# A hybrid decoder step on one core: sample tokens on a path of their own, the paged attention spread over the stages, key pages turned by VectorE

## What is computed

```python
def _conv_layer(x, state, g, w_in, w_conv, w_out):              # layer A
    b, c, u, z = jnp.split(_rmsnorm(x, g) @ w_in, 4, axis=-1)
    v = c * u
    ext = jnp.concatenate([state.astype(v.dtype), v], axis=1)
    ...
    y = (jax.nn.silu(z) * b * conv) @ w_out
    return x + y, ext[:, -(CONV_W - 1):]

def _fox_attend(q, fq, qpos, k, v, fk, kpos):
    s = jnp.einsum('nqhd,nkhd->nhqk', q, k).astype(jnp.float32) * (HEAD_DIM ** -0.5)
    s = s + (jnp.transpose(fq, (0, 2, 1))[:, :, :, None]
             - jnp.transpose(fk, (0, 2, 1))[:, :, None, :])
    ...
    p = jax.nn.softmax(s, axis=-1)
    return jnp.einsum('nhqk,nkhd->nqhd', p.astype(v.dtype), v)

def _fox_layer(x, attend, g, w_in, g_q, w_out):                 # layer B
    q, z = jnp.split(_rmsnorm(x, g) @ w_in, 2, axis=-1)
    q = _rmsnorm(q.reshape(N, L, N_HEADS, HEAD_DIM), g_q)
    o = attend(q).reshape(N, L, D_ATTN)
    return x + (o * jax.nn.silu(z)) @ w_out
```

## Time and profile before

| | |
|---|---|
| time, median of 3 runs | 976.64 us (974.82 to 976.98) |
| span of the profiled execution | 973.7 us; its own time is not listed apart, the median lies 2.9 us above the span |
| TensorE, matmuls | 935.6 us busy, 8516 instructions |
| VectorE, ScalarE, GpSimd | 489.1, 384.8, 168.3 us busy |
| moved by DMA | 206.4 MB, 212 GB/s on average |

### The profile page before, as it was taken

The page is one execution under the profiler, slowest core; times in us unless marked ns, Lnnn a source line. Parts: engine busy times, 40 slices in busy tenths (PEclk is TensorE's granted clock), DMA queues, the critical chain, the costliest instruction groups (busy, mean ns, idle before and its releaser), DMA issues.

```text
span 973.7 us, 23729 instructions
## 1 busy us (share of the span) xinstructions
PE 935.6 (96%) x8516; PEld 798.8 (82%) x8516; DVE 489.1 (50%) x1133; ACT 384.8 (40%) x728; POOL 168.3 (17%) x111
## 2 busy tenths in 40 slices
PE   3899999999999999999999999999999999999998
PEld 2899999999998997758768768678687687786898
DVE  5744645555256434453554544644535545545732
ACT  5233333332135443453543544535435445436210
POOL 2243444331130221101102002012020020100000
PEclk8799999999999999999999999999999999999999
DMA  6222222322542525879799799798897997986412
GB/s 211 68 85 86 66 87 84 86 86 89 152 150 81 177 87 178 295 253 368 249 334 335 241 361 317 245 372 297 280 356 251 352 336 241 370 317 227 166 44 98
DMA packets 133188, 206.40 MB, mean 212 GB/s; under 512 B 8831, under 2 KB 91312, under 8 KB 133026
## 3 DMA queue, kind: packets, MB, share of 16 engines
q1 hardware_dynamic: 123538, 199.40, 60.7%
q10 hardware_dynamic: 9088, 4.46, 1.7%
q0 software_dynamic: 528, 2.10, 0.8%
HBM read 195.29 MB, written 10.63 MB: 211 GB/s over the span
## 4 chain that ended last, share of the span: by engine, by line
PE 84%; DMA 5%; DVE 4%; ACT 4%; issue 2%; SPq 0%; ACTq 0%; DVEq 0%
PE psum L1224 41%; PE psum L1194 17%; PE psum L1249 9%; PE psum L1382 7%; PE psum L1497 4%; DMA page_ring<-in_cache_k 4%; ACT sample_scores L708 2%; PE psum L1447 2%; DMA w_raw<-in_a_w_out 1%; PE psum L1425 1%; PE psum L1297 1%; PE psum L1405 1%; PE psum L1427 1%; PE psum L1429 1%; DMA constants<-in_table 0%
## 5 line engine op out<-in xcount | busy, mean ns | idle before, releaser
L1224 PE MATMUL psum<-xn_high,w_high 128*128 128x256 f32 x992 | 233.9, 318 | 2.6 <-DVE xn_low L821 2.6
L1224 PE MATMUL psum<-xn_low,w_high 128*128 128x256 f32 x992 | 213.6, 297 | 0.0
L1224 PE MATMUL psum<-xn_high,w_low 128*128 128x256 f32 x992 | 213.5, 297 | 0.0
L1224 PEld LDWEIGHTS psum<-xn_high,w_high 128*128 128x128 f32 x992 | 162.9, 191 | 19.6 <-issue 16.6
L1224 PEld LDWEIGHTS psum<-xn_high,w_low 128*128 128x128 f32 x992 | 168.1, 190 | 0.0
L1224 PEld LDWEIGHTS psum<-xn_low,w_high 128*128 128x128 f32 x992 | 168.0, 190 | 0.0
L1194 PE MATMUL psum<-constants,page_ring 128*128 128x128 f32 x1024 | 136.4, 276 | 6.3 <-DMA page_ring<-in_cache_k 5.0
L1194 PEld LDWEIGHTS psum<-constants,page_ring 128*128 128x128 f32 x1024 | 114.1, 140 | 33.4 <-issue 31.9
L503 POOL TENSOR_TENSOR w_raw<-w_raw,gains 128x1024 f32<-128x1024 f32 x32 | 60.7, 1897 | 339.2 <-DMA w_raw<-in_b_w_in 218.3
L1002 DVE COPY k_turned_odd<-psum 128x512 f32<-128x512 f32 x64 | 44.1, 690 | 93.1 <-PE psum L1194 93.1
L835 DVE TENSOR_TENSOR w_low<-w_raw,w_high 128x1024 fp32r<-128x1024 f32 x32 | 49.6, 1551 | 78.7 <-ACT w_high L565 78.7
(11 more groups left out here) (236 smaller groups left out, 1418.7 us busy)
## 6 DMA issues: line engine op xcount, KB each, us to landing
page_ring<-in_cache_k SPq DMA_DIRECT2D x128, 512.0 KB, 5.6
page_ring<-in_cache_v SPq DMA_DIRECT2D x128, 512.0 KB, 4.7
w_raw<-in_a_w_in SPq DMA_DIRECT2D x32, 512.0 KB, 4.0
suffix<-suffix_scratch SPq DMA_DIRECT2D x32, 256.0 KB, 4.6
w_raw<-in_b_w_in SPq DMA_DIRECT2D x16, 512.0 KB, 5.6
w_raw<-in_kv_w SPq DMA_DIRECT2D x16, 512.0 KB, 6.3
w_raw<-in_a_w_out SPq DMA_DIRECT2D x4, 1024.0 KB, 5.0
f_broad<-f_scratch SPq DMA_DIRECT2D x8, 512.0 KB, 6.0
```

The lines of the kernel that those rows point to most:

```text
L1224: mm = pe.matmul(PS[:, bank + h, 0:c.stop - c.start], w[:, k, :], x[:, k, c], start=(k == 0 and n == 0), stop=(k == KT - 1 and n == 2))
```

## The change

The stages stay, but three things are new.

*The samples leave the prompt's matmuls in the mixer and the queries.* Their rows are now the stationary side: `weights_s` streams 48 weight blocks of 128x1024 (A's input, A's output, the queries' weights) in plain fp32 against 64 columns, ahead of and between the prompt's first channels. So the queries of all samples are there before the mixer's third channel. The prompt's pieces become one matmul of 512 columns. In the heads, key, value and gate projections still run over 576.

*The paged attention follows at once*: sequences 0 to 2 in channels 2 to 7 of the mixer, sequence 3 in the queries, 4 to 7 one for each two pairs of heads. The ring has 16 slots; a value page takes the slot of its key page when that is done with.

*Key pages are turned in place by VectorE*, in blocks of 32x32, and the scores are matmuls on 32x32 tiles that work on these blocks. ScalarE spreads the queries (`spread`).

```diff
--- before.py
+++ after.py
@@ TensorE
-                for p in range(4):
-                    mm = turn(PS[:, T0, p * P:(p + 1) * P], page[:, p * P:(p + 1) * P])
...
+        def weights_s(n, bank):
+            pe.wait_ge(b_page[n % RING], 16 * (n // RING + 1))
+            for h in range(2):
+                mm = pe.matmul(PS[64 * h:64 * h + 64, bank, :], XT[:, n % KT, :], ring[:, n % RING, h * WIDE:(h + 1) * WIDE],
+                               start=(n % KT == 0), stop=(n % KT == KT - 1))
...
+        def piece_a(slot, k, bank):
+            for n, (w, x) in enumerate(((WH, XH), (WH, XL), (WL, XH))):
+                mm = pe.matmul(PS[:, bank, :], w[:, slot, k, :], x[:, k, 0:SEQ],
+                               start=(k == 0 and n == 0), stop=(k == KT - 1 and n == 2))
...
+        def past_scores(r):
+            for h in range(4):
+                for a in range(2):
+                    for j in range(4):
+                        for g in range(4):
+                            c = ((4 * j + h) * 2 + a) * 32
+                            mm = pe.matmul(
+                                PS[32 * j:32 * j + 32, T0 + g, 0:ROUND * 32].rearrange("p (n k) -> p n k", k=32),
+                                QC[32 * g:32 * g + 32, j, 64 * h + 32 * a:64 * h + 32 * a + 32],
+                                ring[32 * g:32 * g + 32, ROUND * r:ROUND * r + ROUND, c:c + 32],
+                                start=(h == 0 and a == 0), stop=(h == 3 and a == 1), tile_position=(32 * g, 32 * j))
...
+        def mixer(i, b):
+            channel(i, 0, range(KT - 1))
+            past_free(b, 0)
+            channel(i, 0, [KT - 1])
+            past_scores(0)
+            channel(i, 1)
+            channel(i, 2, range(KT - 1))
+            past_free(b, 1)
+            channel(i, 2, [KT - 1])
+            past_scores(1)
+            channel(i, 3)
+            past_turns(b)
+            channel(i, 4)
+            past_out(b, range(ROUND), T0, 256)
+            channel(i, 5)
+            past_out(b, range(ROUND, NPG), T0, 256)
...
+                project(e, 0, 0, [5])
+                block_scores(o, 1, 1)
+                project(e, 0, 0, [6, 7])
+                block_turn(o, 0)
+                block_scores(o, 2, 1)
+                project(e, 1, 1, [0, 1])
+                block_out(o, 0)
+                block_turn(o, 1)
@@ VectorE
+        def turn_pages(b, pages):
+            for n in pages:
+                dve.wait_ge(b_page[n], 32 * b + 16 * (S_LOADS + 1))
+                dve.transpose(ring[:, n, :], ring[:, n, :]).then_inc(b_turned, 1)
...
+        def mixer(i, b):
+            turn_pages(b, range(ROUND, 12))
+            take_scores(b, 0)
+            conv(i)
+            turn_pages(b, range(12, NPG))
+            take_scores(b, 1)
...
+                attend(e - 1, (pages(8), keys_e, pages(11, 12), pages(13)))
+                turn_pages(b, (14, 15))
@@ GpSimd
+        def low_b(n, odd, to=None):
+            h, lo = to or (WH[:, odd, :, :], WL[:, odd, :, :])
+            pool.wait_ge(b_high, n + 1)
+            pool.tensor_tensor(lo, WR[:, odd, :, :], h.bitcast(F32), ALU.subtract).then_inc(b_split, 1)
...
+        pool.wait_ge(b_used, NPG * NB)
+        pool.memset(QZ[:, :, :, :], 0.0).then_inc(s_zero, 1)
```

More of the change, by code:

```diff
@@ new lines, in _, with mixer @@
+        spread(0)
+        ahead(0, 6)
+        silu_a(1)
+        ahead(0, 7)
+        gated_high(1)
+        def mixer(i, b, last):
+            ahead(i, 0, last)
+            c_out(i)
+            ahead(i, 1, last)
+            ahead(i, 2, last)
+            silu_a(i)
+            exps(b)
+            ahead(i, 3, last)
+            gated_high(i)
+            probs_out(b)
+            ahead(i, 4, last)
+            c_out(i + 1)
+            spread(b + 1)
+            ahead(i, 5, last)
+            past_out(b, OUT_M)
+            ahead(i, 6, last)
+            silu_a(i + 1)
+            if last:
+                act.wait_ge(l_raw, 16)
+                high_slab(0)
+            ahead(i, 7, last)
+            gated_high(i + 1)
@@ new lines, in _ @@
+        act.wait_ge(s_wfl, 1)
+        for n in (2, 3):
+            load_b(n, n % 2, wqz, n * P)
+        for m in range(KT):
+            query(m)
+            if m == 4:
+                probs_out(3)
+            query_root(m)
+            if m + 4 < KT:
+                load_b(m + 4, m % 2, wqz, (m + 4) * P)
+            elif m + 4 < KT + 2:
+                load_b(m + 4, m % 2, wkv, (0, D)[m % 2])
+            if m == 3:
+                exps(3)
+                spread(4)
+        act.wait_ge(b_proj, KT - 1)
@@ new lines, in _ @@
+        channel(0, 1)
+        pe.wait_ge(y_dve, Y_DVE["ext"])
+        pe.wait_ge(s_cs, H)
+        pe.matmul(PS[:, S_BANK[1], 0:H], CT[:, C_TRI:C_TRI + P], CS[:, :, PAGE - 1], start=True, stop=True).then_inc(s_rtot, 1)
+        pe.wait_ge(y_dve, Y_DVE["gate"])
+        turn_s(S_BANK[2], ZG).then_inc(y_pe, 1)
+        channel(0, 2, range(4))
+        pe.wait_ge(y_dve, Y_DVE["gated"])
+        for n in range(S_IN, S_IN + S_OUT):
+            weights_s(n, S_BANK[0])
+        channel(0, 2, range(4, KT))
@@ L1503, in _, with piece @@
-        with pe.Fori(0, NB) as i:
-            heads(i)
+        past_out(3, range(ROUND), OS, 0)
+        query(6)
+        past_out(3, range(ROUND, NPG), OS, 0)
+        query(7)
+        q_sum(7)
+        pe.wait_ge(q_out, KT)
+        pe.wait_ge(s_fnr, 1)
+        def piece(slot, k):
+            for n, (w, x) in enumerate(((WH, XH), (WH, XL), (WL, XH))):
+                for h in range(2):
+                    c = (slice(0, HALF), slice(HALF, TOK))[h]
+                    mm = pe.matmul(PS[:, D0 + h, 0:c.stop - c.start], w[:, slot, k, :], x[:, k, c],
+                                   start=(k == 0 and n == 0), stop=(k == KT - 1 and n == 2))
+            return mm
```

2142 lines of the change are left out of this document (1260 added, 882 removed).

## The result

| | before | after |
|---|---|---|
| time, median | 976.81 us (974.82 to 977.72) | 1129.8 us (1124.77 to 1136.42) |
| span of the profiled execution | 973.7 | 1130.2 |
| ratio after/before, 95% interval | | 1.1566 [1.1533, 1.1598] |

The change makes the kernel 15.7% slower. The forecast was 965 us with a range up to 1030; it was wrong, in size and in sign. Nothing failed in what the change does: TensorE's page turns are gone and its busy time fell, from 935.6 to 904.4 us. What makes 1130 is TensorE's idle time, 226 us in all (before: 38), and a lower granted clock.

The account below looks back on a forecast made before the run. The prediction took TensorE, busy 935.6 of 973.7 us, as the bound. Its work would fall to about 804 us while idle time rose from 38 to 158; stages summed to 962, with 3 around it 965 us, range 885 to 1030.

Parts of the forecast that it names:

- Page turns: TensorE's work: the 1024 matmuls that turn 128 key pages go, 111 us less.
- sample columns: TensorE's 40 mixer and query projections: one matmul of 512 columns for each piece saves 38 us.
- the samples' path: New TensorE work: 48 weight blocks against 64 stationary columns, at 0.9 us each, 43 us more.
- Scores, 64 us: Paged attention on TensorE: 16 rounds of 128 matmuls on 32x32 tiles, 4.0 us each, 64 us as before.
- Rival E: Score rounds: tiles don't overlap, a round is 16 us, 192 us more; 1155 us, chance 0.04.
- the low clock, charged once with 2.5 us: Start stage: after 9 us idle behind the suffix sums, 12 pieces run at the lower clock, 2.5 us.
- The list of waits: TensorE's waits for other engines, laid out stage by stage: idle time goes from 38 to 158 us.
- Block turn 0: Heads: TensorE waits 6.5 us in a pair for VectorE's divide, which follows maxima, keys' gain and pages.
- Page turn 1.14 us: VectorE's turn of a 128x1024 fp32 key page takes 1.14 us, with bounds of 0.75 to 2.16.
- Rival B: VectorE's page turns run in the fast form at 0.81 us, giving back 19 us; 945 us, chance 0.12.
- Rival C: VectorE's page turns slow beside GpSimd, costing 26 us at 1.55 or 65 at 2.16; 995 us, chance 0.25.
- Rival A: Waits are shorter because queues run ahead, 158 us of idle time becomes 80; 885 us, chance 0.22.

Follow-up runs that it names:

- e3: The changed kernel with each score matmul streaming 128 columns instead of 256, half of the pages' scores left out: 1127.9 us, ratio 1.151 to the kernel before.
- e9: The changed kernel with the score round's tile order swapped, four column groups of one row group one after the other: 1129.1 us, ratio 1.156 to the kernel before.
- e7: The changed kernel with 20 and 22 useless matmuls ahead of the waits for pages and block turn 0: 1121.8 us, ratio 1.149 to the kernel before.
- g1: The changed kernel with three orders turned: division of block 0 earlier, ScalarE's probability copies earlier, page turns 12 to 15 ahead of the convolution: 1098.9 us, ratio 1.120.
- e1: The changed kernel with VectorE's division of block 0 ahead of the keys' gain and page turns 9 and 10: 1097.7 us, ratio 1.121 to the kernel before.
- e4: The changed kernel with 64 instead of 128 matmuls in a score round, part of the scores left out: 1066.2 us, ratio 1.092 to the kernel before.
- e8: The changed kernel with VectorE turning only the first 32 columns of each key page: 1115.2 us, ratio 1.144 to the kernel before.
- e5: The changed kernel with GpSimd making only one eighth of each weight's low half: 1105.6 us, ratio 1.133 to the kernel before.
- b1: The kernel before the change with each 256-column score matmul cut in four of 64, same results: 1036.8 us, ratio 1.061.
- b2: The kernel before the change with each 256-column score matmul cut in two of 128: 981.6 us, ratio 1.005.

## Why the prediction was wrong, point by point

- *Page turns, sample columns, the samples' path.* Right. A piece of 512 columns comes every 0.227 us; 48 blocks cost 49 us for 43. TensorE's work at the full clock is 832 us for 804.
- *Scores, 64 us, "below this it cannot well go".* Mis-sized: 99.6 us, part of it at the low clock; at the full clock a round takes 5.9 us, 23 ns a record for the 16 of the earlier trace rows. That row has 64 columns a matmul; here there are 256, and e3 shows that columns count on these tiles too. The 3.4 us "if columns alone count" come out for 128 matmuls four at a time; by the 256 records the same sum is 6.9. Rival E had named the tiles, with four at a time, 62 ns a record; the 23 lie between. The rule of the Trainium skill that it goes by (TensorE: Matmul & The Clock Gate, Part 3: Packing small matmuls: a weight load overlaps matmuls in flight only where the row group differs) has no support here: e9 puts four column groups of one row group after each other and takes the same 99.7 us.
- *The first step that failed: the low clock, charged once with 2.5 us.* It is the largest part of the 168 us. The clock was low in 36 separate stretches, most of them behind 2 to 8 us of idleness, 73 us in all. The row that says so was the earlier trace rows, and I applied it to one stretch only, though my own list had 156 us of idle time. e7 shows that the low clock follows the idle stretches; how much time comes back without it, no run shows clearly.
- *The second: idle time is what engines wait for each other.* The list of waits had no place for code and put it at nothing. It is 33 us of issue in the changed kernel, nearly all of it behind instruction packets, and more where other waits go: 21 us more of it in g1 than in e1. Rows of before show none of it, since their loop's body is kept (20 packets); I did not count that a body now holds two heads' work, 2330 records for 1310, with 512 of them in each round of 6 us. The rest of the idle time, 193 us, is 37 more than the list had. e4's 64 us are not all part of the miss: 32 of them would have gone by the forecast's own price of the rounds too.
- *Waits in the list.* Block turn 0: 6.5 forecast, 7.8 measured. The page turns are a small part of it (e8: 54 to 47 us over all pairs) and the division, three times as long beside GpSimd, a larger one (e5: 54 to 43); the keys wait 2.0 us for ScalarE's squares, as forecast. Second score round 3.8 and 5.6; the suffix stores' 9 us were a wait of 5.3 near 86 us; spread queries 12 and 11.1; copies of probabilities in a heads pair 4.4 and 2.9.
- *Page turn 1.14 us.* Right: 1.13 from start to start. Rival B's 19 us for the fast form go by 0.4 us a page, where 1.14 less 0.81 is 0.33, so 16.
- *Rival C, pages slow beside GpSimd.* Right side, wrong operation. Turns don't slow; the divisions do (1.62 us on average for 512 columns, 0.48 before), as does one step of the convolution with one input, also 128x512 (2.64 us beside it, 0.49 without). The 2.5 us a page that this rival works out from the Trainium skill (VectorE: DVE Perf Modes, The three transpose paths) did not come: that table's figure is for a 16-bit type, which the prediction does not say, and the fp32 turns took 1.2 us. GpSimd's low half is itself 2.4 us where I took 2.
- *Rival A and the range.* The range ended at 1030, as no case joined the low clock to all waits. That alone, 70 us more on 965, gives 1035.

## What to carry to other kernels

Before trading a few large matmuls for many small ones, count instructions as well as columns: per round, and per loop body. If the body before has few instruction packets and no issue time, it says nothing about a larger one; cutting one group of matmuls finer, results unchanged, tests it in one run (b1). When TensorE's work is cut but idle stretches appear, charge the low clock behind each one of them, and expect a removed wait to uncover the next floor. An idle gap without a releaser is not yet a wait for code: look whether an instruction packet lands in it, and whether another engine ends something just before it does.

## What the runs showed of the hardware

- A loop body of TensorE with 1570 matmul and load records was kept (b2: 21 instruction packets for the run); one with 1697 was fetched anew at each turn (9 packets a turn in the changed kernel's mixer); with 2080, 93 packets came and each turn of the loop stood 5.4 to 6.0 us (b1). Gaps of over 1 us in which TensorE waited for code ended 1.2 to 1.8 us after a packet had landed.
- On 32x32 tiles a record of 256 columns took 23 ns, in either order of row and column groups (e9), and one of 128 took 14 (e3).
- VectorE's 32x32 block transpose of 128x1024 fp32 took 1.19 to 1.25 us, also beside GpSimd; two divisions of 128x512 with one tensor input took 2.56 us beside it and 0.88 without.
- Matmuls of no use inside waits cut the low clock's cost from 73 to 50 us (e7); the kernel's time fell by 8, within the noise.
